# Token mixing: the normalised activations of successive tiles alternate between two buffers

## Chip, cores and metric

One Trainium2 chip; the kernel runs on 8 of its cores, and each core computes half of one batch element's tokens (4 batches, 2 halves). Nothing is exchanged between the cores. The metric is the device time in microseconds of the slowest core. Before the change it is 3632.73 us, the median of 3 runs (3630.87 to 3634.38).

## What is computed

The reference is a two-layer backbone. Each layer is a SwiGLU feed-forward, a token-mixing stage and a second feed-forward, each preceded by an RMS norm with scale and shift. Cut to the part that matters here, the mixing stage:

```python
n = norm_modulate(h, norm_mix[l], mx[:, 3], mx[:, 4])      # rmsnorm(h)*(1+scale)+shift
u, q, k, v = split(n @ w_in, [512, 1024, 1152])            # u 512, q 512, k 128, v 128 columns
pool_out = pool_mixer(u, w_pool, pool_scale)               # windowed means of u, minus u
q, k = apply_rope(q, cos, sin), apply_rope(k, cos, sin)
attn_out = latent_attention(q, k, v, kc, vc, sink)         # window of 128, plus context, plus sink
h = h + mx[:, 5] * (concat([pool_out, attn_out], -1) @ w_out)
```

Context tokens go through the same stage with their own scale and shift, so that a tile of columns can hold tokens of both kinds.

## The kernel before

The residual stream h lies in SBUF, transposed: 8 chunks (k) of 128 channels by 2560 token columns (2304 latent, 256 context). The program is a list of stages with a barrier over all engines between them; per layer they are feed-forward 1, the mixing stage (function mix), feed-forward 2. A small scheduler class records operations in the order in which the code is written, one queue for each engine, and derives semaphore waits from the names that an operation reads and writes. An engine executes its queue strictly in that order, so the order in the code is the order on each engine.

The change lies in the first phase of mix, called phase A here. It walks over five column tiles: four of 512 columns and a last one of 512 in layer 0 and 384 in layer 1. For each tile TensorE (PE) needs the normalised activations of all 8 chunks, kept in the buffer nTt (8 x 512, bf16). One tile's main steps are ten:

- 4 steps utok_step (u of 128 tokens: 8 matmuls of 512 columns, evacuated in turn by ScalarE, L513, and VectorE, L515), called **u blocks** here;
- 2 steps k_step (16 matmuls of 512 columns each, and then three VectorE operations L534, L536, L538 for the rotary embedding, called a **rope** here);
- 4 steps v_step (8 matmuls of 128 columns, evacuated by ScalarE, L547).

The last tile of layer 1 has three of the blocks of 128 tokens instead of four.

The normalisation of a tile is written as small steps. Eight **square** steps: a ScalarE square of one chunk (L346) and one PE matmul with a matrix of ones that adds up the channels, 512 columns. One **rstd** step: two ScalarE operations, Ln (L352) and Exp (L354). Then the **mod** steps: a VectorE multiplication h x rstd into one of two fp32 buffers tmp (L378), and a ScalarE operation that scales and shifts it into nTt (L380). There is one mod per chunk and kind of token: 8 in a tile of 512 latent columns, 24 in the last tile of layer 0 (latent, context, latent), 16 in the last tile of layer 1.

interleave(main, side) writes a main step, then a few side steps, then the next main step. Before the change the side list holds the 9 square and rstd steps of the next tile, one after each main step; the next tile's mods are written after the last main step, since they overwrite the only nTt that the v steps still read:

```python
                interleave(main, rn)
                for st in mn:
                    st()
```

After phase A comes the pooling phase: matmuls of u with the constant matrices in the buffer band (32 x 128, bf16, the same 8 KB per partition as nTt). Band is loaded by a DMA of POOL's queue at the head of the phase, behind the two loads of win (wkv, then wu), and is first read by the pooling phase.

Of the kernel before, what the change touches and what calls it, by code (L numbers as in the profile page):

```python
# [178 lines left out]
def build(upto="final", dump=False):  # L179
# [3 lines left out]
    with es:  # L183
        S = Sched(nc, es)

        def din(name, shape):
            return nc.dram_tensor(name, list(shape), F32, kind="ExternalInput").ap()
# [16 lines left out]
        bandT = din("bandT", [128, 32, 128])  # L204
# [45 lines left out]
        nTt = alloc(BF16, [8, 512], dma=True)  # L250
# [24 lines left out]
        band = alloc(BF16, [32, 128], dma=True)  # L275
# [90 lines left out]
        def norm_steps(c0, n, i_norm, dst, dst_keys, eng="dve", split=False):  # L366
            rsteps = rstd_steps(c0, n)
            steps = []
            shift_i = 3 * i_norm
            par = curp["par"]  # L370
            modraw, Amod = modraw_l[par], Amod_l[par]

            def mod_step(k, a, m, t):
                off = a - c0
                ti = cnt["tmp"] % 2
                cnt["tmp"] += 1
                tmp = tmp_s[ti]
                S.op(eng, lambda e: e.tensor_tensor(tmp[:, 0:m], hT[:, k, a:a + m], rstd[:, off:off + m], ALU.mult),  # L378
                     reads=hkeys(k, a, m) + [("rstd",)], writes=[("tmp", ti)])
                S.op("act", lambda e: e.activation(  # L380
                    dst(k, off, m), tmp[:, 0:m], AF.Identity, bias=modraw[:, shift_i * 8 + k, t:t + 1],
                    scale=Amod[:, i_norm, k, t:t + 1]),
                    reads=[("tmp", ti), ("modraw", par, shift_i), ("Amod", par, i_norm)], writes=dst_keys(k))

            for k in range(8):
                for (a, m, t) in colset_ranges(c0, n):
                    steps.append(lambda k=k, a=a, m=m, t=t: mod_step(k, a, m, t))
            if split:
                return rsteps, steps
            return rsteps + steps  # L390
# [5 lines left out]
        def interleave(main, side):  # L396
            side = list(side)
            nm = max(len(main), 1)
            per = (len(side) + nm - 1) // nm
            for st in main:  # L400
                st()
                for _ in range(per):
                    if side:
                        side.pop(0)()
            while side:
                side.pop(0)()
# [82 lines left out]
        def mix(l):  # L489
# [12 lines left out]

            S.dma("pool", None, wkv, win[l, :, :, 512:WCA], writes=[("wkv",)])
            S.dma("pool", None, wu, win[l, :, :, 0:512], writes=[("wu",)])
            S.dma("pool", None, band, bandT, writes=[("band",)])
            S.op("dve", lambda e: e.memset(Vaug[:, :, :, 64:128], 1.0), writes=[("Vaug",)])
            acols = [(0, 512), (512, 512), (1024, 512), (1536, 512), (2048, 384) if last else (2048, 512)]
            ev_i = [0]
# [5 lines left out]
                else:  # L514
                    S.op("dve", lambda e: e.tensor_copy(dst, src), reads=reads, writes=writes)  # L515

            def a_norm(c0, n):
                return norm_steps(c0, n, 1, lambda k, o2, m: nTt[:, k, o2:o2 + m], lambda k: [("nTt", k)], eng="dve", split=True)

            nk = [("nTt", k) for k in range(8)]  # L520
            r0, m0 = a_norm(*acols[0])
            for st in r0 + m0:
                st()
            for ti, (c0, n) in enumerate(acols):
                def cs_load(n=n, c0=c0):
                    S.dma("sp", None, cst[:, 0, 0:n], cosT[:, c0:c0 + n], writes=[("cs", 0)])
                    S.dma("sp", None, cst[:, 1, 0:n], sinT[:, c0:c0 + n], writes=[("cs", 1)])

                def k_step(g, n=n, c0=c0):
                    S.mm(pa[g][:, 0:n], [(wkv[:, k, g * 128:(g + 1) * 128], nTt[:, k, 0:n]) for k in range(8)],  # L530
                         reads=[("wkv",)] + nk, writes=[("pa", g)])
                    S.mm(pb[g][:, 0:n], [(wkv[:, k, 256 + g * 128:256 + (g + 1) * 128], nTt[:, k, 0:n]) for k in range(8)],
                         reads=[("wkv",)] + nk, writes=[("pb", g)])
                    S.op("dve", lambda e: e.tensor_tensor(rt[0][:, 0:n], pa[g][:, 0:n], cst[:, 0, 0:n], ALU.mult),  # L534
                         reads=[("pa", g), ("cs", 0)], writes=[("rt", 0)])
                    S.op("dve", lambda e: e.tensor_tensor(rt[1][:, 0:n], pb[g][:, 0:n], cst[:, 1, 0:n], ALU.mult),  # L536
                         reads=[("pb", g), ("cs", 1)], writes=[("rt", 1)])
                    S.op("dve", lambda e: e.tensor_tensor(kT[:, g, c0:c0 + n], rt[0][:, 0:n], rt[1][:, 0:n], ALU.add),  # L538
                         reads=[("rt", 0), ("rt", 1)], writes=[("kT", g, c0)])

                def v_step(tb, c0=c0):
                    blk = (c0 + tb * 128) // 128
                    pi = cnt["p"] % 2
                    cnt["p"] += 1
                    S.mm(py[pi][:, 0:128], [(nTt[:, k, tb * 128:(tb + 1) * 128], wkv[:, k, 512:640]) for k in range(8)],
                         reads=[("wkv",)] + nk, writes=[("py", pi)])
                    S.op("act", lambda e: e.copy(  # L547
                        Vaug[:, blk, :, 0:64], py[pi][:, 0:128].rearrange("p (g d) -> p g d", g=2)),
                        reads=[("py", pi)], writes=[("Vaug",)])

                def utok_step(tb, c0=c0):
                    blk = c0 // 128 + tb
                    pi = cnt["p"] % 2
                    cnt["p"] += 1
                    S.mm(py[pi][:, :], [(nTt[:, k, tb * 128:(tb + 1) * 128], wu[:, k, :]) for k in range(8)],
                         reads=[("wu",)] + nk, writes=[("py", pi)])
                    evac(utok[:, blk, :], py[pi][:, :], [("py", pi)], [("utok", blk)])

                cs_load()
                nb_ = n // 128  # L560
                main = [lambda tb=tb: utok_step(tb) for tb in range(nb_)]
                main += [lambda g=g: k_step(g) for g in range(2)]
                main += [lambda tb=tb: v_step(tb) for tb in range(nb_)]
                if ti + 1 < len(acols):
                    rn, mn = a_norm(*acols[ti + 1])
                else:
                    rn, mn = [], []
                interleave(main, rn)
                for st in mn:
                    st()  # L570
            oblocks = list(range(16)) if last else list(range(19))
            for t0 in range(0, len(oblocks), 4):
                obs = oblocks[t0:t0 + 4]
                n = 128 * len(obs)
# [96 lines left out]
            for ti, (c0, n) in enumerate(qtiles):  # L671
                S.dma("sp", None, cst[:, 0, 0:n], cosT[:, c0:c0 + n], writes=[("cs", 0)])
                S.dma("sp", None, cst[:, 1, 0:n], sinT[:, c0:c0 + n], writes=[("cs", 1)])
                nk = [("nTt", k) for k in range(8)]
# [38 lines left out]
                side = q_norm(*qtiles[ti + 1]) if ti + 1 < len(qtiles) else []  # L713
# [213 lines left out]
```

How the kernel before makes its waits and increments, by code:

```python
    def _waits(self, eng, d):  # L72
        seen = self.seen[eng]
        for s, v in d.items():
            if seen.get(s, 0) < v:
                seen[s] = v
                h = self.sems[s]
                self.ops[eng].append(lambda e, h=h, v=v: e.wait_ge(h, v))
# [10 lines left out]
    def op(self, eng, fn, reads=(), writes=()):  # L89
        self._waits(eng, self._deps(reads, writes))
        sname = "s_" + eng
        h = self.sem(sname)
        self.cnt[sname] += 1
        ev = (sname, self.cnt[sname])
        self.ops[eng].append(lambda e, fn=fn, h=h: fn(e).then_inc(h, 1))
        self.nins[eng] += 1
        self._commit(ev, reads, writes)
# [1 line left out]
    def mm(self, out, pairs, reads, writes, start=True, stop=True):  # L99
# [1 line left out]
        h = self.sem("s_pe")  # L101
        self.cnt["s_pe"] += 1
        ev = ("s_pe", self.cnt["s_pe"])
        n = len(pairs)
        for i, pr in enumerate(pairs):
            l, r = pr[0], pr[1]
            o_i = pr[2] if len(pr) > 2 else out
            st_i = pr[3] if len(pr) > 3 else (start and i == 0)
            sp_i = pr[4] if len(pr) > 4 else (stop and (i == n - 1))
            if i == n - 1:
                self.ops["pe"].append(lambda e, l=l, r=r, o_i=o_i, st_i=st_i, sp_i=sp_i: e.matmul(o_i, l, r, start=st_i, stop=sp_i).then_inc(h, 1))
            else:
                self.ops["pe"].append(lambda e, l=l, r=r, o_i=o_i, st_i=st_i, sp_i=sp_i: e.matmul(o_i, l, r, start=st_i, stop=sp_i))
        self.nins["pe"] += n
```

## Time and profile before

| what | value |
|---|---|
| median of 3 runs | 3632.73 us |
| the profiled execution, its own time | 3629.62 us |
| its span on the slowest core (core 3) | 3628.0 us |
| spans of the eight cores | 3610.2 to 3628.0 us |
| PE busy, share of the span | 3060.3 us, 84% |
| ACT busy (ScalarE) | 1096.0 us, 30% |
| DVE busy (VectorE) | 838.5 us, 23% |
| mean granted TensorE clock, core 3 | 0.924 |

PE is the matmul engine, PEld its weight load, ACT ScalarE, DVE VectorE, POOL GpSimd, SP the queue of plain DMAs. In a timeline a row is: start in us, us of the row's time, engine, line of the kernel, operation, destination <- source with shape, xcount, and in brackets the idle time of that engine before it with what ended it. Most tiles are called arena (SBUF) or ps (PSUM) by the profile, since the kernel carves them from one allocation each; lines tell them apart. All matmuls are recorded by one helper: L113 are those inside an accumulation group, L111 the last one of each group. A clock of 1.0 is 2.4 GHz and 0.5 is 1.2 GHz. In layer 0 phase A runs from about 735 to 927 us of the span, in layer 1 from about 2565 to 2740 us.

### The profile page before, as it was taken

What the parts mean: (1) busy time and instruction counts of PE and PEld (TensorE: products, weight loads), DVE (VectorE), ACT (ScalarE), POOL (GpSimd) and SP (SyncE); (2) the same over time, 40 slices, a digit from 0 to 9 for tenths busy, and PEclk for the clock granted to TensorE, in tenths of its full rate; (3) what the DMA queues carried; (4) which work ended last, traced back from release to release, by engine and by line L of the source; (5) the groups of instructions that cost most, each with busy time, mean ns of one, the idle gap of its engine ahead of it and who ended that gap; (6) DMA issues with size and microseconds to landing.
All of it is one profiled execution on the core that took longest, in us unless ns stands there. A gap on an engine that the chain in (4) does not pass through costs nothing.

```text
span 3628.0 us, 50030 instructions; the slowest of 8 cores (3610.2 to 3628.0 us)
## 1 busy us (share of the span) xinstructions
PE 3060.3 (84%) x17532; PEld 1545.9 (43%) x17532; DVE 838.5 (23%) x1491; ACT 1096.0 (30%) x1936; POOL 392.6 (11%) x560
## 2 busy tenths in 40 slices
PE   0799999955678877999998899999655888799997
PEld 0355555522333434555554454555323343344442
DVE  0212222123122222122122222221231222212113
ACT  0412311034345643122111313210343565312112
POOL 1011000000022220100100000000001322000000
PEclk9899999977589988999999999999886999899998
DMA  8565344230110004643743232343302000353444
GB/s 186 77 100 94 66 73 69 49 54 18 23 37 12 5 17 73 107 83 69 121 88 58 47 60 53 65 69 68 63 16 53 13 7 1 53 88 69 65 77 126
DMA packets 75957, 224.14 MB, mean 62 GB/s; under 512 B 9156, under 2 KB 14532, under 8 KB 74184
## 3 DMA queue, kind: packets, MB, share of 16 engines
q0 software_dynamic: 63328, 192.24, 31.6%
q1 hardware_dynamic: 12392, 28.70, 2.5%
q8 instruction: 153, 2.51, 0.3%
q14 instruction: 84, 0.69, 0.1%
HBM read 404.74 MB, written 8.39 MB: 114 GB/s over the span
## 4 chain that ended last, share of the span: by engine, by line
PE 73%; ACT 10%; issue 5%; DMA 5%; DVE 4%; POOL 3%; ACTq 0%; DVEq 0%; SPq 0%; POOLq 0%
PE ps L113 62%; PE ps L111 11%; ACT arena L634 3%; ACT arena L380 3%; POOL arena L686 2%; DMA arena<-win 2%; DVE arena L378 2%; DMA arena<-wmod 1%; ACT arena L651 1%; ACT arena L346 1%; DMA arena<-cT 1%; DMA arena<-wab 1%; DVE arena L682 1%; DMA arena<-wo 1%; DVE arena L723 0%
## 5 line engine op out<-in xcount | busy, mean ns | idle before, releaser
L113 PE MATMUL ps<-arena 128*128 128x512 bf16 (+3 forms) x15146 | 2813.8, 330 | 326.5 <-ACT arena L380 103.5
L113 PEld LDWEIGHTS ps<-arena 128*128 128x128 bf16 x15146 | 1349.1, 100 | 1567.5 <-issue 461.3
L111 PE MATMUL ps<-arena 128*128 128x512 bf16 (+3 forms) x2386 | 785.4, 341 | 230.8 <-ACT arena L346 186.8
L452 ACT ACTIVATE arena<-ps 128x512 f32<-128x512 f32 (+2 forms) x484 | 255.7, 529 | 1170.2 <-PE ps L111 1162.8
L454 DVE TENSOR_TENSOR arena<-arena,ps 128x512 bf16<-128x512 f32 (+2 forms) x484 | 291.4, 603 | 1151.6 <-PE ps L111 1114.0
L111 PEld LDWEIGHTS ps<-arena 128*128 128x128 bf16 x2386 | 237.9, 100 | 503.7 <-issue 368.2
L413 DVE SCALAR_TENSOR_TENSOR arena<-ps,arena 128x512 f32<-128x512 f32 (+3 forms) x288 | 175.3, 620 | 672.0 <-PE ps L111 672.0
L380 ACT ACTIVATE arena<-arena 128x512 bf16<-128x512 f32 (+3 forms) x392 | 265.3, 705 | 191.4 <-DVE arena L378 146.4
L346 ACT ACTIVATE arena<-arena 128x512 bf16<-128x512 f32 (+3 forms) x360 | 182.4, 579 | 318.2 <-DVE arena L413 199.3
L634 ACT ACTIVATE arena<-ps 128x512 bf16<-128x512 f32 x334 | 176.3, 598 | 202.9 <-PE ps L111 201.5
L378 DVE TENSOR_TENSOR arena<-arena 128x512 f32<-128x512 f32 (+3 forms) x312 | 164.4, 543 | 193.3 <-ACT arena L354 129.1
L131 POOL DMA_DIRECT2D arena<-wab x176 | 93.9, 534 | 891.5 <-PE ps L111 770.4
L131 POOL DMA_DIRECT2D arena<-wmod x144 | 76.8, 534 | 668.2 <-PE ps L111 656.3
L378 POOL TENSOR_TENSOR arena<-arena 128x512 f32<-128x512 f32 (+1 forms) x80 | 88.0, 1131 | 295.4 <-ACT arena L354 290.9
L658 DVE TENSOR_TENSOR arena<-ps,arena 64x256 bf16<-64x256 f32 x140 | 58.4, 417 | 264.7 <-ACT arena L652 257.4
L131 POOL DMA_DIRECT2D arena<-wo x64 | 33.9, 532 | 705.7 <-PE ps L111 705.7
L686 POOL TENSOR_TENSOR arena<-arena 64x512 bf16<-64x512 f32 (+1 forms) x72 | 88.6, 1230 | 112.5 <-DVE arena L682 109.8
L515 DVE CAST arena<-ps 128x512 bf16<-128x512 f32 (+1 forms) x37 | 25.3, 685 | 211.6 <-PE ps L111 211.6
L500 ACT ACT_TABLE_LOAD x2 | 2.6, 1283 | 191.3 <-DMA arena<-sinkrow 191.3
L131 POOL DMA_DIRECT2D arena<-win x6 | 5.3, 890 | 457.3 <-ACT arena L346 457.3
L680 DVE TENSOR_TENSOR arena<-ps,arena 128x512 f32<-128x512 f32 (+1 forms) x36 | 24.4, 677 | 122.1 <-POOL arena L686 76.0
L513 ACT CAST arena<-ps 128x512 bf16<-128x512 f32 (+1 forms) x38 | 22.0, 580 | 91.6 <-PE ps L111 91.5
(32 smaller groups left out, 314.7 us busy)
## 6 DMA issues: line engine op xcount, KB each, us to landing
arena<-wab POOLq DMA_DIRECT2D x176, 512.0 KB, 6.3
arena<-wo POOLq DMA_DIRECT2D x64, 704.0 KB, 6.6
arena<-wmod POOLq DMA_DIRECT2D x144, 256.0 KB, 5.2
arena<-xT SPq DMA_DIRECT2D x8, 1280.0 KB, 25.3
outT<-arena SPq DMA_DIRECT2D x32, 256.0 KB, 2.2
arena<-cosT SPq DMA_DIRECT2D x17, 256.0 KB, 2.7
arena<-sinT SPq DMA_DIRECT2D x17, 256.0 KB, 2.7
arena<-win POOLq DMA_DIRECT2D x2, 2048.0 KB, 17.2
```

Of the source, the lines that this page charges most:

```text
L111: self.ops["pe"].append(lambda e, l=l, r=r, o_i=o_i, st_i=st_i, sp_i=sp_i: e.matmul(o_i, l, r, start=st_i, stop=sp_i).then_inc(h, 1))
L113: self.ops["pe"].append(lambda e, l=l, r=r, o_i=o_i, st_i=st_i, sp_i=sp_i: e.matmul(o_i, l, r, start=st_i, stop=sp_i))
L131: self.ops[eng].append(lambda e: e.dma_start(out=out, in_=in_).then_inc(h, 16))
L346: S.op("act", lambda e: e.activation(sqr[si][:, 0:n], hT[:, k, c0:c0 + n], AF.Square), reads=hkeys(k, c0, n), writes=[("sq", si)])
L378: S.op(eng, lambda e: e.tensor_tensor(tmp[:, 0:m], hT[:, k, a:a + m], rstd[:, off:off + m], ALU.mult), reads=hkeys(k, a, m) + [("rstd",)], ...
L380: S.op("act", lambda e: e.activation(dst(k, off, m), tmp[:, 0:m], AF.Identity, bias=modraw[:, shift_i * 8 + k, t:t + 1], scale=Amod[:, i_n ...
L413: S.op("dve", lambda e, a=a, m=m, t=t, o2=o2: e.scalar_tensor_tensor(hT[:, d, a:a + m], pst[1][:, o2:o2 + m], gate[:, i_norm, d, t:t + 1], ...
L452: S.op("act", lambda e, pi=pi, n=n: e.activation(sa_s[pi][:, 0:n], pa[pi][:, 0:n], AF.Silu), reads=[("pa", pi)], writes=[("sa", pi)])
L454: S.op("dve", lambda e, pi=pi, n=n, j=j, off=off: e.tensor_tensor(gTb[:, j, off:off + n], sa_s[pi][:, 0:n], pb[pi][:, 0:n], ALU.mult), rea ...
L634: S.op("act", lambda e, stp=stp, pti=pti: e.activation(PT[pti], stp[:, :], AF.Exp, scale=0.125), reads=[stkey], writes=[("PT", pti)])
L658: S.op("dve", lambda e, i0v=i0v, i1v=i1v, ov=ov: e.tensor_tensor(ov, i0v, i1v, ALU.mult), reads=[pvkey, ("rt", 0)], writes=[("aot", 2 * g) ...
L686: S.op("pool", lambda e, c=c, n=n, hf=hf, rows=rows: e.tensor_tensor(qz[rows, 2 * c + hf, 0:n], rt[0][rows, 0:n], rt[1][rows, 0:n], ALU.ad ...
```

## The change

The tiles alternate between two buffers: even tiles are normalised into nTt as before, odd tiles into nTt2, which is the memory of band seen as 8 x 512. The next tile's normalisation, all of it, becomes the side list of the present tile: 17 steps over ten main steps, so two after each main step until they are used up; 33 in the last transition of layer 0 (four after each) and 25 in that of layer 1 (three after each). The load of band moves behind the tile loop. Its writers and readers of the odd tiles share one name, ("band",), where nTt has one name per chunk.

```diff
-            S.dma("pool", None, band, bandT, writes=[("band",)])
...
-            def a_norm(c0, n):
-                return norm_steps(c0, n, 1, lambda k, o2, m: nTt[:, k, o2:o2 + m], lambda k: [("nTt", k)], eng="dve", split=True)
+            nTt2 = band.rearrange("p a b -> p (a b)").rearrange("p (k c) -> p k c", k=8)
+            nbufs = [nTt, nTt2]
+
+            def nkeys(ti):
+                return [("nTt", k) for k in range(8)] if ti % 2 == 0 else [("band",)]
+
+            def a_norm(ti, c0, n):
+                nb = nbufs[ti % 2]
+                return norm_steps(c0, n, 1, lambda k, o2, m: nb[:, k, o2:o2 + m],
+                                  (lambda k: [("nTt", k)]) if ti % 2 == 0 else (lambda k: [("band",)]), eng="dve")
...
-                if ti + 1 < len(acols):
-                    rn, mn = a_norm(*acols[ti + 1])
-                else:
-                    rn, mn = [], []
-                interleave(main, rn)
-                for st in mn:
-                    st()
+                side = a_norm(ti + 1, *acols[ti + 1]) if ti + 1 < len(acols) else []
+                interleave(main, side)
+            S.dma("pool", None, band, bandT, writes=[("band",)])
```

The matmuls of k, v and u read whichever of the two buffers holds their tile. Three places show what moves. On VectorE, the rows of the first tile of layer 0 before the change: two evacuations of u (L515), two ropes (L534, L536, L538), then the eight multiplications of the next tile's mods (L378).

```order
L515 CAST arena<-ps 128x512 x2
L534 TENSOR_TENSOR arena<-ps,arena 128x512
L536 TENSOR_TENSOR arena<-ps,arena 128x512
L538 TENSOR_TENSOR arena<-arena 128x512
L534 TENSOR_TENSOR arena<-ps,arena 128x512
L536 TENSOR_TENSOR arena<-ps,arena 128x512
L538 TENSOR_TENSOR arena<-arena 128x512
L378 TENSOR_TENSOR arena<-arena 128x512 x8
```

The same place with the change (the lines are 1 lower for the evacuation, L514, and 7 higher for the rope, L541, L543, L545):

```order
L514 CAST arena<-ps 128x512 x2
L541 TENSOR_TENSOR arena<-ps,arena 128x512
L543 TENSOR_TENSOR arena<-ps,arena 128x512
L545 TENSOR_TENSOR arena<-arena 128x512
L378 TENSOR_TENSOR arena<-arena 128x512
L541 TENSOR_TENSOR arena<-ps,arena 128x512
L543 TENSOR_TENSOR arena<-ps,arena 128x512
L545 TENSOR_TENSOR arena<-arena 128x512
L378 TENSOR_TENSOR arena<-arena 128x512 x7
```

One mod stands between the two ropes; seven still stand behind the second rope. On ScalarE, the same tile with the change (L512 evacuates u, L554 v):

```order
L512 CAST arena<-ps 128x512
L346 ACTIVATE arena<-arena 128x512 x4
L512 CAST arena<-ps 128x512
L346 ACTIVATE arena<-arena 128x512 x4
L352 ACTIVATE arena<-ps,arena 128x512
L354 ACTIVATE arena<-arena 128x512
L380 ACTIVATE arena<-arena 128x512 x3
L554 CAST arena<-ps 128x2x64
L380 ACTIVATE arena<-arena 128x512 x2
L554 CAST arena<-ps 128x2x64
L380 ACTIVATE arena<-arena 128x512 x2
L554 CAST arena<-ps 128x2x64
```

Before, the squares stood as 2, 4, 1 and 1 between the evacuations, and all eight L380 behind the fourth evacuation of v. Now all eight squares come in the four u blocks, and the evacuations of v stand among the mods. On POOL the load of band keeps its place in the queue and gets waits for ScalarE and PE:

```order
L131 DMA arena<-win 128x8x640
L131 DMA arena<-win 128x8x512
L131 DMA arena<-bandT 128x4096 [waits s_act,s_pe]
```

Before, the third of these rows had no wait. The waits are for the last mod into band and the last matmul that reads it, the fourth v step of the fourth tile.

## Rows read from the trace of the kernel before

**Rows 1.** The page's head.

```profile
span 3628.0 us, 50030 instructions; the slowest of 8 cores (3610.2 to 3628.0 us)
```

**Rows 2.** Busy time by stage: second, fourth, last tile (layer 0), fourth, last (layer 1).

```profile
core 3: us, PE busy (x) PEld busy (x) DVE busy (x) ACT busy (x) POOL busy (x), PEclk, DMA share, GB/s
798.20:832.26 34.06, 20.40 (x105) 9.66 (x105) 10.99 (x16) 13.61 (x24) 0.00 (x0) 0.80 0.05 16
866.33:908.67 42.34, 20.33 (x104) 9.56 (x105) 13.53 (x32) 20.01 (x40) 0.00 (x0) 0.74 0.05 13
908.67:927.30 18.63, 18.46 (x95) 8.64 (x96) 5.54 (x8) 1.82 (x5) 0.00 (x0) 0.85 0.00 1
2689.86:2725.85 35.99, 19.19 (x105) 9.12 (x106) 10.94 (x24) 14.43 (x32) 0.00 (x0) 0.83 0.04 11
2725.85:2739.97 14.12, 13.96 (x81) 7.31 (x81) 4.04 (x7) 1.70 (x4) 0.00 (x0) 0.85 0.00 0
```

**Rows 3.** Waits in phase A of layer 0: us in total, times, longest.

```profile
PE ps L113 <- ACT arena L380: 44.1, 4, 17.2
```

**Rows 4.** Timeline of PE, second tile of layer 0, and the third tile's start.

```profile
798.20 3.15 PE L113 MATMUL ps<-arena 128*128 128x512 bf16 x7 [9.20 <-ACT arena L380]
...
803.09 0.38 PE L111 MATMUL ps<-arena 128*128 128x512 bf16 x1 [1.35 <-ACT arena L346]
...
810.65 1.67 PE L113 MATMUL ps<-arena 128*128 128x512 bf16 x7
...
814.32 1.67 PE L113 MATMUL ps<-arena 128*128 128x512 bf16 x7
...
832.26 3.14 PE L113 MATMUL ps<-arena 128*128 128x512 bf16 x7 [8.85 <-ACT arena L380]
```

**Rows 5.** Timeline of ScalarE in the same tile.

```profile
801.83 0.58 ACT L513 CAST arena<-ps 128x512 bf16<-128x512 f32 x1 [3.88 <-PE ps L111]
802.31 1.15 ACT L346 ACTIVATE arena<-arena 128x512 bf16<-128x512 f32 x2
...
822.71 0.27 ACT L547 CAST arena<-ps 128x128 bf16<-128x128 f32 x1 [1.30 <-PE ps L111]
822.87 0.69 ACT L352 ACTIVATE arena<-ps,arena 128x512 f32<-128x512 f32 x1
...
825.17 1.52 ACT L380 ACTIVATE arena<-arena 128x512 bf16<-128x512 f32 x2 [0.74 <-DVE arena L378]
```

**Rows 6.** Timeline of VectorE in the same tile.

```profile
812.72 0.69 DVE L534 TENSOR_TENSOR arena<-ps,arena 128x512 f32<-128x512 f32 x1 [1.32 <-PE ps L111]
...
815.24 0.69 DVE L538 TENSOR_TENSOR arena<-arena 128x512 bf16<-128x512 f32 x1
...
818.84 0.69 DVE L538 TENSOR_TENSOR arena<-arena 128x512 bf16<-128x512 f32 x1
824.38 1.29 DVE L378 TENSOR_TENSOR arena<-arena 128x512 f32<-128x512 f32 x2 [4.85 <-ACT arena L354]
826.16 1.40 DVE L378 TENSOR_TENSOR arena<-arena 128x512 f32<-128x512 f32 x2 [0.48 <-ACT arena L380]
```

**Rows 7.** VectorE: first mod of the last tile, layer 0, then layer 1.

```profile
892.45 0.63 DVE L378 TENSOR_TENSOR arena<-arena 128x128 f32<-128x128 f32 x2 [4.76 <-ACT arena L354]
...
2714.60 0.63 DVE L378 TENSOR_TENSOR arena<-arena 128x128 f32<-128x128 f32 x2 [4.17 <-ACT arena L354]
```

**Rows 8.** PE in the first tile of layer 0: second u block, fourth v step.

```profile
767.22 3.19 PE L113 MATMUL ps<-arena 128*128 128x512 bf16 x7
...
787.94 0.95 PE L113 MATMUL ps<-arena 128*128 128x128 bf16 x7
```

**Rows 9.** Timeline, first tile of layer 0: its last mods, its first matmuls.

```profile
755.58 1.52 ACT L380 ACTIVATE arena<-arena 128x512 bf16<-128x512 f32 x2 [0.25 <-DVE arena L378]
...
761.81 3.14 PE L113 MATMUL ps<-arena 128*128 128x512 bf16 x7 [14.01 <-DMA arena<-win]
```

**Rows 10.** DMA issues, 735 to 770 us: count, KB each, us to landing.

```profile
arena<-bandT POOLq DMA_DIRECT2D x1, 1024.0 KB, 24.3
```

**Rows 11.** The page's DMA issues: the nearest smaller load of POOL's queue.

```profile
arena<-wo POOLq DMA_DIRECT2D x64, 704.0 KB, 6.6
```

More of the change, by code:

```diff
@@ L515, in evac @@
                     S.op("dve", lambda e: e.tensor_copy(dst, src), reads=reads, writes=writes)
-            def a_norm(c0, n):
-                return norm_steps(c0, n, 1, lambda k, o2, m: nTt[:, k, o2:o2 + m], lambda k: [("nTt", k)], eng="dve", split=True)
-            nk = [("nTt", k) for k in range(8)]
-            r0, m0 = a_norm(*acols[0])
-            for st in r0 + m0:
+            nTt2 = band.rearrange("p a b -> p (a b)").rearrange("p (k c) -> p k c", k=8)
[6 more added lines that the diff above has]
+                                  (lambda k: [("nTt", k)]) if ti % 2 == 0 else (lambda k: [("band",)]), eng="dve")
+            for st in a_norm(0, *acols[0]):
                 st()
             for ti, (c0, n) in enumerate(acols):
+                nTt_ = nbufs[ti % 2]
+                nk = nkeys(ti)
                 def cs_load(n=n, c0=c0):
@@ L527, in cs_load, with k_step @@
                     S.dma("sp", None, cst[:, 1, 0:n], sinT[:, c0:c0 + n], writes=[("cs", 1)])
-                def k_step(g, n=n, c0=c0):
+                def k_step(g, n=n, c0=c0, nTt=nTt_, nk=nk):
                     S.mm(pa[g][:, 0:n], [(wkv[:, k, g * 128:(g + 1) * 128], nTt[:, k, 0:n]) for k in range(8)],
@@ L539, in k_step, with v_step @@
                          reads=[("rt", 0), ("rt", 1)], writes=[("kT", g, c0)])
-                def v_step(tb, c0=c0):
+                def v_step(tb, c0=c0, nTt=nTt_, nk=nk):
                     blk = (c0 + tb * 128) // 128
@@ L549, in v_step, with utok_step @@
                         reads=[("py", pi)], writes=[("Vaug",)])
-                def utok_step(tb, c0=c0):
+                def utok_step(tb, c0=c0, nTt=nTt_, nk=nk):
                     blk = c0 // 128 + tb
```

## The prediction, made before the changed kernel ran

> **What bounds the kernel now.** I read the page's head first, then the waits of phase A, then its time by stage, and last one tile engine by engine. The span is 3628.0 us on the slowest core [rows 1], and the change touches phase A alone, twice. There the view of waits has one entry that the change can remove: before four tiles of layer 0, PE's first matmul waits for the next tile's last mod, 44.1 us in all, 17.2 the longest [rows 3]. Tiles are serial: a regular transition takes 34.06 us, of which PE is busy 20.40; the transition into the last tile takes 42.34 in layer 0 and 35.99 in layer 1 [rows 2]. In the timeline PE stands 9.20 and 8.85 us before two tiles [rows 4], while VectorE and ScalarE work off eight mods: from 824.38 [rows 6] to 832.26 [rows 4], 7.88 us. A pair of mods takes 826.16 - 824.38 = 1.78 us, so one takes 0.89: two tmp buffers make VectorE and ScalarE alternate.
>
> **A regular transition, step by step.** There are six (three per layer). All offsets are from the tile's first matmul, 798.20 [rows 4].
>
> *The front gets later.* After a u block, ScalarE evacuates it, squares, and PE's matmul with ones waits for that: 1.35 us [rows 4]. With two squares per block PE waits for the second one too. Two squares take 1.15 us, the first about 0.6, so the second adds 0.53 [rows 5]. ScalarE evacuates two of the four blocks, so this happens twice; behind the other two the squares are ready. Further, four ones matmuls move ahead of the k steps, two of them without any wait to hide in: 17 matmuls take 814.32 - 810.65 = 3.67 us, 0.216 each [rows 4]. Together 2 x 0.53 + 2 x 0.216 = 1.5 us: the first k step moves from offset 12.45 (810.65) to 13.95. The second follows after 16 matmuls instead of 17, 3.46 us later: 17.41.
>
> *The ropes.* The first rope ends 815.24 + 0.69 - 810.65 = 5.28 us after its k step's start [rows 4, 6], at 19.23. The one mod that now stands between the ropes fits there: rstd is ready 824.38 - 822.87 = 1.51 us after Ln starts [rows 5, 6], and Ln can start at about 14.2, behind the last ones matmul, so at 15.7. It delays the second rope's first operation by half a microsecond, but not its second, which waits for PE anyway. The second rope ends 818.84 + 0.69 - 814.32 = 5.21 us after its k step [rows 4, 6]: 22.62.
>
> *The tail.* Seven mods remain: from 22.7, 7 x 0.89 = 6.2 plus what the eight of before took beyond 8 x 0.89 (0.76) is 7.0, so 29.7. Two things may stretch this. ScalarE's mods into band now each wait for the one before (one name for all chunks), and three evacuations of v stand among them. From below: nothing, since in a cycle of 1.78 a pair keeps ScalarE busy for 1.52 [rows 5]. From above: three evacuations at 0.25 each, 0.75, as one takes 0.27 [rows 5]. I take 0.3, nearer the first, because the pair's slack holds one evacuation. The next tile starts at 30.0 instead of 34.06: **4.06 us gained, six times: 24.4.** PE's third and fourth v step now wait for evacuations behind mods, which costs nothing: they end before the last mod.
>
> **The last transitions.** Layer 0: four squares stand behind each of the first two u blocks. The evacuation starts at 3.63 (801.83), takes 0.58, four squares 2.2, so PE resumes at 6.75; a u block (1.73) and four ones matmuls (0.86) bring 9.34, the third block 11.07, its evacuation 11.9, rstd 13.4. From there VectorE works off the train of 24 mods, 908.67 - 892.45 = 16.22 us [rows 2, 7], with one evacuation (0.69) and six rope operations (4.5 with gaps) put into it: 34.8, less 0.4 where VectorE need not wait for ScalarE behind an interruption: 34.4. **42.34 - 34.4 = 7.9.** Layer 1: the first mod stands behind the fourth u block's evacuation, about offset 14.6; the train is 2725.85 - 2714.60 = 11.25 us [rows 2, 7], with the same six rope operations 30.4, a little less for the same reason, 30.3. **35.99 - 30.3 = 5.7.** I allow 0.8 either way on each. The first tile's own normalisation and the last tile's matmuls keep their order: nothing.
>
> **The load of band**, moved. Behind nothing but its wait in POOL's queue, it is issued after the fourth tile's fourth v step. That step waits for an evacuation that stands five mods (layer 0) or four (layer 1) ahead of the last: about 31.2 and 28.0. The last tile takes 18.63 and 14.12 us [rows 2] from 34.4 and 30.3, so the load has some 21.8 and 16.4 us. Its price alone is in no row. From below 6.6 us, as a smaller load of that queue took [rows 11]; from above 24.3, band's own landing behind two loads of win [rows 10]. I take about 9, since nothing else is in that queue then: hidden by the last tile, nothing to pay. At the upper end 2.5 + 7.9 = 10.4 us would show. At the phase's head band no longer follows win: PE's start there waits for win until 761.81 though the mods end at 757.10 [rows 9], so at most 4.7 us, and 5.0 with a little in layer 1; at least nothing, which I take, as band was issued behind win.
>
> The load's descriptors are now made beside VectorE's casts. The Trainium skill (SBUF — State Buffer, Who interferes with whom) says that some casts and copies take the port pair that GpSimd needs, so that a load issued by POOL stands still behind them. No row here shows such a stall; by the rule the load is late by part of VectorE's work. For a bound from rows: all of that work in the last tile of layer 0 is 5.54 us [rows 2], and 9 + 5.5 still lands in time.
>
> **The clock.** Each tile starts at 1.2 GHz: seven matmuls of 512 columns take 3.15 us against 1.67 later [rows 4]. In the first tile of layer 0 the second u block was at 1.2 GHz too, 3.19 [rows 8]: 1.5 us more. The wait behind the first block grows by half a microsecond, so some more second blocks may start at 1.2 GHz. Eight tiles (four per layer) have that wait; on this core only the one shown did so. Bounds: none more, or all seven others: 10.6. I take two more, as the wait grows by less than half: 3.0 us lost. The first block stays at 1.2 GHz: the fourth v step was at that level after two waits of some 1 us (0.95 us for seven short matmuls) [rows 8], and from the third v step to the next tile PE will again do almost nothing. The Trainium skill (TensorE: Matmul & The Clock Gate, HAM oscillation) says that an idle stretch which is short enough leaves the clock up. By that rule the shorter stretch could start tiles at 2.4 GHz; that is the second rival.
>
> **Sum.** 24.4 + 7.9 + 5.7 - 3.0 = 35.0. The profiled execution took 3629.6 us, so 3594.6; the median of the three runs is 3.1 above it, so **3598 us** (-1.0%). No later stage gets other work or another order, so nothing is given back there.
>
> **Rivals.**
> 1. *The whole tile at 1.2 GHz (slower than before).* If the longer waits keep the clock down through all u and k blocks, 56 of a tile's 64 matmuls of 512 columns take 0.21 us more (1.48 / 7), 11.8 us per tile; eight tiles 94 us against 38 gained: 3689. It decides from some 23 extra slow matmuls per tile. Against it: 32 matmuls of the k steps follow without a wait. For it: only that two long waits stand in each tile.
> 2. *Tiles start at 2.4 GHz.* Each of the eight transitions gains another 8 x 0.21 = 1.7, and the 3.0 lost fall away: 38 + 13.5 = 51.5 gained: 3581. Against it: [rows 8].
> 3. *Band lands late*, 10.4 us in all: 3608. For it: eight cores load at the same time; against: nothing stands in front of it in its queue.
> 4. *The second u block is slow in every tile*: 7.6 us less gain, 3605.
> 5. *The change does not do what it says*: seven of eight mods still stand behind the second rope. If ScalarE's queue (evacuations, waits on its own mods) stretches each mod by 0.5 us, 3.5 us per regular transition, about all is eaten: six times 3.5 is 21, leaving 14: 3619. Against it: the slack of 0.25 per pair.
>
> **How the numbers follow.** About 0.2% (7.3 us) is what a measurement can tell from no change. Chances: forecast 0.70, rival 1 0.03, rival 2 0.08, rival 3 0.07, rival 4 0.08, rival 5 0.04. The forecast's own range: up by 0.3 x 6 = 1.8, 1.6, 3.0 and 5.0 to 3587; down by 2.7, 1.6 and 7.6 to 3610. To hold 8 in 10, with rivals 3 and 4 inside, I give 3583 to 3612. All but rival 1 are faster by over 0.2%; with a little for what I don't see: faster 0.94, same 0.03, slower 0.03.
>
> **What would show it.** Right: a regular transition of 30 us, the last ones 34 and 30; one L378 between the ropes, then seven; PE's waits for L346 twice per tile, about 1.9 us; PE's wait for the last mod down from 8.9 to some 2 us; no wait of PE for bandT. Wrong: u or k blocks at 3.1 us throughout, a wait for bandT before the pooling phase, mods at more than 0.9 us each, or a tile whose k steps start later than offset 14.5.

## The result, and the profile after

The changed kernel takes 3595.29 us (median), the kernel before, run beside it, 3632.74. Four of the nine runs behind this median, and two of the ten before, were slowed by a lower granted clock on one die or on both; the ratio, taken from the others (3592.84 to 3595.29 us after the change), is 0.9896, with a 95% interval from 0.9883 to 0.9908: 1.04% faster. 3598 had been predicted, and 3594.6 for the profiled execution, which took 3594.31.

The page's head, which answers to [rows 1], and the busy time:

```profile
span 3592.7 us, 50089 instructions; the slowest of 8 cores (3574.6 to 3592.7 us)
...
PE 3071.0 (85%) x17532; PEld 1545.4 (43%) x17532; DVE 835.5 (23%) x1491; ACT 1095.2 (30%) x1936; POOL 392.6 (11%) x560
```

The slowest core is now core 6; before it was core 3. What follows is core 3's, as in [rows 2 to 7], unless another is named. The span of core 3 fell from 3628.0 to 3588.1, 39.9 us, and the mean over the eight cores from 3619.7 to 3584.8, 34.9. Core 6 gained less than core 3: from 3626.2 to 3592.7.

Busy time by stage, to be read beside [rows 2]: the second and the fourth tile of layer 0, the fourth and the last tile of layer 1. The columns are those of [rows 2].

```profile
789.01:818.77 29.76, 21.02 (x104) 9.67 (x105) 10.71 (x16) 13.45 (x24) 0.00 (x0) 0.84 0.07 18
850.01:882.79 32.78, 20.94 (x104) 9.80 (x105) 12.66 (x32) 19.47 (x40) 0.55 (x1) 0.81 0.06 17
2655.65:2685.62 29.97, 20.75 (x105) 9.72 (x106) 10.37 (x24) 14.29 (x32) 0.55 (x1) 0.84 0.05 14
2685.62:2699.80 14.18, 13.96 (x75) 7.02 (x75) 3.94 (x7) 1.62 (x4) 0.00 (x0) 0.83 0.40 75
```

The engines do the same work in less time: 34.06 became 29.76, 42.34 became 32.78, 35.99 became 29.97. The last tile, 14.12 before, stayed at 14.18. All eight transitions of core 3, from the first matmul of a tile to that of the next:

| transition | before | after | gained |
|---|---|---|---|
| layer 0, first | 36.39 | 30.14 | 6.25 |
| second | 34.06 | 29.76 | 4.30 |
| third | 34.07 | 31.24 | 2.83 |
| last | 42.34 | 32.78 | 9.56 |
| layer 1, first | 34.36 | 29.58 | 4.78 |
| second | 34.05 | 29.79 | 4.26 |
| third | 34.20 | 31.28 | 2.92 |
| last | 35.99 | 29.97 | 6.02 |
| sum | 285.46 | 244.54 | 40.9 |

The sum is core 3's whole gain in span, 39.9, and one more. Over the eight cores the transitions shrank by 37.5 us on average, the spans by 34.9. So the gain lies in the transitions. Most of the other 2.6 us are given back in the next phase of the stage, where PE waits for its own load of win (the q columns). Core 3 in layer 0, before and after:

```profile
1003.94 3.15 PE L113 MATMUL ps<-arena 128*128 128x512 bf16 x7 [15.29 <-DMA arena<-win]
979.91 3.14 PE L113 MATMUL ps<-arena 128*128 128x512 bf16 x7 [17.34 <-DMA arena<-win]
```

Over the eight cores PE's wait at this place grew from 13.9 to 15.8 us on average in layer 0 and from 12.9 to 13.7 in layer 1, in one profiled execution each; where win is early, it is 12.5 and ends with the phase's own mods. Why it grew was not tried.

The waits of PE in phase A of layer 0, after (us in total, times, longest):

```profile
PE ps L113 <- ACT arena L554: 28.9, 12, 6.2
PE ps L111 <- ACT arena L346: 17.2, 8, 7.7
PE ps L113 <- DMA arena<-win: 13.5, 1, 13.5
```

The entry of [rows 3], 44.1 us of waiting for mods, is gone by name. In its place the profile has twelve waits for evacuations of v (L554), which now stand between and behind the mods in ScalarE's queue. Eight of the twelve, 21.5 us, are those of the third and fourth v steps. The other four, 7.4 us, stand at the starts of tiles, and there the name misleads: by the code a tile's first u block needs the last mod, but not the last evacuation. ScalarE at the end of the second tile, before and after:

```profile
830.49 1.52 ACT L380 ACTIVATE arena<-arena 128x512 bf16<-128x512 f32 x2 [0.25 <-DVE arena L378]
...
817.71 0.81 ACT L380 ACTIVATE arena<-arena 128x512 bf16<-128x512 f32 x1
818.43 0.25 ACT L554 CAST arena<-ps 128x128 bf16<-128x128 f32 x1
```

PE starts the next tile 0.25 us after the end of the last mod, in the kernel before (832.01, 832.26) as with the change (818.52, 818.77), and so at the other tile starts of this core. So the tiles are still serial, and PE still waits for the last mod, but 7.4 us instead of 44.1. The waits for squares (L346) are fewer too: 17.2 us in 8 times, where the kernel before had 28.1 in 17.

PE in the second tile of layer 0, the tile of [rows 4]:

```profile
789.01 3.14 PE L113 MATMUL ps<-arena 128*128 128x512 bf16 x7 [1.94 <-ACT arena L554]
...
793.93 0.90 PE L111 MATMUL ps<-arena 128*128 128x512 bf16 x2 [1.35 <-ACT arena L346]
794.73 1.67 PE L113 MATMUL ps<-arena 128*128 128x512 bf16 x7
...
803.03 1.67 PE L113 MATMUL ps<-arena 128*128 128x512 bf16 x7
...
806.48 1.67 PE L113 MATMUL ps<-arena 128*128 128x512 bf16 x7
...
814.31 0.91 PE L113 MATMUL ps<-arena 128*128 128x128 bf16 x7 [3.32 <-ACT arena L554]
...
816.08 0.91 PE L113 MATMUL ps<-arena 128*128 128x128 bf16 x7 [0.76 <-ACT arena L554]
...
818.77 3.15 PE L113 MATMUL ps<-arena 128*128 128x512 bf16 x7 [1.68 <-ACT arena L554]
```

The first k step starts at offset 14.02 (803.03), the second at 17.47 (806.48). Before the next tile PE waits 1.68 us where it had waited 8.85. VectorE in the same tile, to be read beside [rows 6]:

```profile
807.62 0.69 DVE L545 TENSOR_TENSOR arena<-arena 128x512 bf16<-128x512 f32 x1
808.23 0.68 DVE L378 TENSOR_TENSOR arena<-arena 128x512 f32<-128x512 f32 x1
808.83 0.68 DVE L541 TENSOR_TENSOR arena<-ps,arena 128x512 f32<-128x512 f32 x1
...
811.00 0.69 DVE L545 TENSOR_TENSOR arena<-arena 128x512 bf16<-128x512 f32 x1
811.61 1.29 DVE L378 TENSOR_TENSOR arena<-arena 128x512 f32<-128x512 f32 x2
...
816.92 0.69 DVE L378 TENSOR_TENSOR arena<-arena 128x512 f32<-128x512 f32 x1 [0.37 <-ACT arena L380]
```

One mod stands between the ropes, and it costs the second rope nothing. That rope ends at 811.69, offset 22.68, and the other seven mods follow at once; before, VectorE idled 4.85 us there for rstd [rows 6]. From the rope's end to the next tile is 7.08 us. The load of band, in the DMA issues of layer 0, answers to [rows 10]:

```profile
arena<-bandT POOLq DMA_DIRECT2D x1, 1024.0 KB, 9.9
```

POOL issues it at offset 31.10, and it lands in 9.9 us. Over all cores and both layers it takes 8.0 to 9.9, fourteen of sixteen loads at most 8.6, and nobody waits for it.

### The profile page after: what moved, and what is told of

It reads as the page before. It is cut to its first block, busy times and chain, and to the rows that moved or that the text cites. A ratio compares the mean times of both kernels' runs of the same rounds, so it can differ in the third digit from the quotient of the medians.

```text
span 3592.7 us, 50089 instructions; the slowest of 8 cores (3574.6 to 3592.7 us)
## 1 busy us (share of the span) xinstructions
PE 3071.0 (85%) x17532; PEld 1545.4 (43%) x17532; DVE 835.5 (23%) x1491; ACT 1095.2 (30%) x1936; POOL 392.6 (11%) x560
## 4 chain that ended last, share of the span: by engine, by line
PE 73%; ACT 9%; issue 5%; DMA 5%; DVE 4%; POOL 3%; ACTq 0%; DVEq 0%; SPq 0%; POOLq 0%
PE ps L113 63%; PE ps L111 10%; ACT arena L637 3%; POOL arena L689 2%; ACT arena L380 2%; DMA arena<-win 2%; DVE arena L378 1%; DMA arena<-wmod 1%; ACT arena L654 1%; DMA arena<-cT 1%; ACT arena L346 1%; DMA arena<-wab 1%; DVE arena L685 1%; DVE arena L726 0%; ACT arena L512 0%
## 5 line engine op out<-in xcount | busy, mean ns | idle before, releaser
L380 ACT ACTIVATE arena<-arena 128x512 bf16<-128x512 f32 (+3 forms) x392 | 267.4, 706 | 233.6 <-DVE arena L378 187.0
L346 ACT ACTIVATE arena<-arena 128x512 bf16<-128x512 f32 (+3 forms) x360 | 180.5, 578 | 317.4 <-PE ps L111 116.4
L378 DVE TENSOR_TENSOR arena<-arena 128x512 f32<-128x512 f32 (+3 forms) x312 | 163.9, 542 | 159.3 <-ACT arena L354 95.6
L378 POOL TENSOR_TENSOR arena<-arena 128x512 f32<-128x512 f32 (+1 forms) x80 | 88.0, 1131 | 294.7 <-ACT arena L354 290.7
L514 DVE CAST arena<-ps 128x512 bf16<-128x512 f32 (+1 forms) x37 | 25.3, 684 | 220.7 <-PE ps L111 220.7
L352 ACT ACTIVATE arena<-ps,arena 128x512 f32<-128x512 f32 (+3 forms) x45 | 29.2, 649 | 77.2 <-PE ps L111 72.5
L512 ACT CAST arena<-ps 128x512 bf16<-128x512 f32 (+1 forms) x38 | 22.0, 579 | 90.6 <-PE ps L111 90.5
```

Source lines behind the costliest of these rows:

```text
L346: S.op("act", lambda e: e.activation(sqr[si][:, 0:n], hT[:, k, c0:c0 + n], AF.Square), reads=hkeys(k, c0, n), writes=[("sq", si)])
L380: S.op("act", lambda e: e.activation(dst(k, off, m), tmp[:, 0:m], AF.Identity, bias=modraw[:, shift_i * 8 + k, t:t + 1], scale=Amod[:, i_n ...
```

## The experiments

The expectations name theories by letter. A: the gain is the order alone, since rstd and one mod come ahead of the second rope and the tile is one serial chain, so that whatever shortens this chain gains again. B: part of the gain lies at the head of the phase, where band no longer follows win in its queue. C: the second buffer as such gains, since a mod need not wait for the last reader of the only one. D: an earlier front gains nothing, since the work behind it sets the end of the tile.

**The load of band alone.** The kernel before, with only that load moved:

```diff
-            S.dma("pool", None, band, bandT, writes=[("band",)])
...
+                if ti == 3:
+                    S.dma("pool", None, band, bandT, reads=[("kT", 1, c0)], writes=[("band",)])
```

> The kernel before, with one part of the change alone: the load of band is issued behind the fourth tile's second rope instead of at the head of phase A; one buffer, the old order of steps. Theory A (the gain is the reordered normalisation): transitions stay at 34.06 and 42.3 us, the first tile starts when win has landed as before, band lands some 8 to 9 us after its issue and nobody waits for it; 3632 us within 4. Theory B (part of the gain comes from the head, where band no longer competes with win): win lands earlier in layer 0, up to 4.7 us, so 3627 to 3629.

Measured: ratio 1.0007 (0.9965 to 1.005). The interval is too wide to exclude the 5.0 us that the prediction had as its upper bound, so the trace has to speak. The DMA issues of layer 0 on the slowest core (core 2):

```profile
arena<-win POOLq DMA_DIRECT2D x1, 1280.0 KB, 15.1
arena<-win POOLq DMA_DIRECT2D x1, 1024.0 KB, 19.3
arena<-bandT POOLq DMA_DIRECT2D x1, 1024.0 KB, 8.3
```

The kernel before shows 15.0 and 20.4 for the two loads of win. In layer 0 PE's wait for win is 13.2 us on average over the eight cores, 14.4 before and 13.3 after the change; the second load lands after 18.6 us instead of 20.0. In layer 1 it lands after 16.6, and 16.4 before. So taking band away from behind win gives about one microsecond in layer 0 and nothing in layer 1. The transitions keep the lengths of before (36.4, 34.1, 34.1 and 42.4 on core 1). B falls but for this microsecond; the next experiment, which has the late load too, has a lower end of the interval of 0.9992, so that 2.9 us are the most that the late load and the second buffer can give together. Band alone in its queue lands in 8.0 to 9.2 us over all cores.

**The second buffer alone.** The changed kernel with the order of before: the mods are written behind the last main step.

```diff
-                side = a_norm(ti + 1, *acols[ti + 1]) if ti + 1 < len(acols) else []
-                interleave(main, side)
+                rn, mn = a_norm(ti + 1, *acols[ti + 1]) if ti + 1 < len(acols) else ([], [])
+                interleave(main, rn)
+                for st in mn:
+                    st()
```

> The changed kernel with both buffers and the late band load, but the order of before: nine side steps among the main steps, the next tile's mods behind the fourth v step. Theory A: rstd is still only ready behind the third v step, so the second buffer frees the mods of nothing but the wait for the fourth v step, less than half a microsecond: regular transitions 33.6 to 34.1 us, the last of layer 0 42 us, 3626 to 3633 us. Rival C (the overwritten buffer was what held the mods back): most of the gain stays, 3595 to 3605 us.

Measured: ratio 1.0005 (0.9992 to 1.0017). VectorE on core 0, second tile of layer 0:

```profile
812.83 0.69 DVE L546 TENSOR_TENSOR arena<-arena 128x512 bf16<-128x512 f32 x1
818.32 1.29 DVE L378 TENSOR_TENSOR arena<-arena 128x512 f32<-128x512 f32 x2 [4.80 <-ACT arena L354]
```

The 4.80 us of idling for rstd are back, and PE stands 9.12 us before the next tile. The transitions of this core in layer 0 are 34.75, 34.31, 34.44 and 42.12. The buffer alone gains nothing: before the change the mods were held by rstd, not by the readers of nTt. It is what allows the other order. C falls.

**One name for eight chunks.** The prediction put 0.3 us per transition on two things, one of them that mods into band wait for each other. Here the odd buffer has one name per chunk, and the load of band writes all of them:

```diff
-            return [("nTt", k) for k in range(8)] if ti % 2 == 0 else [("band",)]
+            return [("nTt", k) for k in range(8)] if ti % 2 == 0 else [("n2", k) for k in range(8)]
...
-                                  (lambda k: [("nTt", k)]) if ti % 2 == 0 else (lambda k: [("band",)]), eng="dve")
+                                  (lambda k: [("nTt", k)]) if ti % 2 == 0 else (lambda k: [("n2", k)]), eng="dve")
...
-            S.dma("pool", None, band, bandT, writes=[("band",)])
+            S.dma("pool", None, band, bandT, writes=[("band",)] + [("n2", k) for k in range(8)])
```

> The changed kernel with one name per chunk for the second buffer, so that a mod into band no longer waits for the mod before it. Theory A (that wait costs a part of a microsecond per transition into band, beside the evacuations of v): the seven mods behind the second rope take 7.2 us into both buffers instead of 7.4 to 7.7 into band and 7.2 into nTt; four transitions, 1 to 2 us in all: 3593 to 3595 us, no difference that a timing shows. Rival: it costs nothing (trains stay as they are). Rival above: it costs 1.2 us each, 5 us in all: 3590 us.

Measured: ratio 0.9886 (0.9844 to 0.9929), which can't be told from the change's 0.9896. ScalarE in core 6, a pair of mods into band, first in the changed kernel:

```profile
845.29 1.72 ACT L380 ACTIVATE arena<-arena 128x512 bf16<-128x512 f32 x2 [2.63 <-DVE arena L378]
```

and with a name per chunk:

```profile
781.83 1.52 ACT L380 ACTIVATE arena<-arena 128x512 bf16<-128x512 f32 x2
```

The second mod of a pair no longer waits for the end of the first, 0.2 us. On this core the stretch from the second rope to the next tile shrinks from 7.30 to 7.08 us where band is the target (in the first tile of layer 0 from 7.65 to 7.44), and stays at 7.08 where nTt is. The wait is real, and worth 0.22 us in four of the eight transitions: 0.9 us, too little to be seen in the time.

**Squares two ahead.** The changed kernel, with each square written two steps ahead of its matmul with ones, and the first two ahead of the tile (sq_act is the ScalarE part of a square step):

```diff
+                if ahead and k + ahead < 8:
+                    sq_act(k + ahead)
...
+            if ahead:
+                steps.insert(0, lambda: [sq_act(j) for j in range(ahead)])
...
+                side = a_norm(ti + 1, *acols[ti + 1], ahead=2) if ti + 1 < len(acols) else []
+                if side:
+                    side.pop(0)()
```

> The changed kernel with ScalarE's squares written two ahead of the matmuls with ones that read them, so that PE finds them ready and does not wait for evacuation and squares behind the first and third u block. Theory A (these waits make the front of a tile later and bring a second u block at 1.2 GHz): the waits of PE for L346 fall away, the first k step starts at offset 10.3 to 10.8 instead of 14 to 15, and the rest follows: regular transitions 26 to 27 us, the last ones 3 us shorter, some 28 to 35 us in all: 3560 to 3568 us. Rival D (ScalarE and VectorE bound the tile, PE's waits are slack): transitions stay within a microsecond of 30 to 31 us, 3590 to 3596 us.

Measured: ratio 0.981 (0.9781 to 0.9838), against 0.9896 for the change. PE on core 4, second tile of layer 0:

```profile
787.16 2.76 PE L113 MATMUL ps<-arena 128*128 128x512 bf16 x6 [2.32 <-ACT arena L569]
789.72 1.48 PE L111 MATMUL ps<-arena 128*128 128x512 bf16 x3
791.00 1.78 PE L113 MATMUL ps<-arena 128*128 128x512 bf16 x7
...
813.98 1.49 PE L113 MATMUL ps<-arena 128*128 128x512 bf16 x3 [2.33 <-ACT arena L569]
```

Both waits of 1.35 us are gone, and the second u block is no longer at 1.2 GHz (1.78 us for seven). This tile takes 26.82 us, 2.94 less than the 29.76 that core 3 took with the change and without a slow second block; twice 1.35 is 2.7. So the front is on the path, as A says, and D falls. The last transition of layer 0 gained only 1.3 us (32.78 to 31.47), where 3 had been expected: there the train of 24 mods sets the end.

**Mods ahead of the ropes.** k_step is split into its matmuls and its rope, and all mods are written between the k matmuls and the v steps:

```diff
-                main += [lambda g=g: k_step(g) for g in range(2)]
-                main += [lambda tb=tb: v_step(tb) for tb in range(nb_)]
...
-                interleave(main, side)
+                interleave([lambda tb=tb: utok_step(tb) for tb in range(nb_)], rn[:8])
+                for st in rn[8:]:
+                    st()
+                for g in range(2):
+                    k_step(g)
+                for st in mn:
+                    st()
+                for tb in range(nb_):
+                    v_step(tb)
+                for g in range(2):
+                    rope(g)
```

> The changed kernel with the next tile's rstd and all its mods written behind the k steps' matmuls but ahead of both ropes and of the v steps; two squares per u block as in the change. Theory A (VectorE's strict order, seven mods behind the second rope, sets the tile): the first mod starts when rstd is ready, at offset 16 to 17 instead of 19 to 23, eight mods take 7.9 to 8.1 us, then the evacuations of v; regular transitions 25 to 26.5 us instead of 29.7 to 31.3, the last of layer 0 unchanged (its train of 24 already started early), that of layer 1 27 to 28; some 31 to 36 us in all: 3559 to 3565 us. Rival D (ScalarE's queue bounds the tile, or the ropes, now later, hold up the next tile): transitions stay at 29 us or more, 3585 to 3596 us.

Measured: ratio 0.9768 (0.9751 to 0.9785); the median, 3548.0 us, lies below what A had expected. PE on core 4, from the end of the first tile of layer 0 to the start of the third:

```profile
784.48 0.55 PE L113 MATMUL ps<-arena 128*128 128x128 bf16 x7 [2.27 <-ACT arena L557]
...
784.92 0.90 PE L113 MATMUL ps<-arena 128*128 128x128 bf16 x7
...
785.75 2.97 PE L113 MATMUL ps<-arena 128*128 128x512 bf16 x7
...
809.11 0.55 PE L113 MATMUL ps<-arena 128*128 128x128 bf16 x7 [1.83 <-ACT arena L557]
...
810.38 1.67 PE L113 MATMUL ps<-arena 128*128 128x512 bf16 x7 [0.22 <-PE ps L111]
```

The order gives what it should: this tile takes 24.63 us. Two things change with it, which this run does not separate: the mods come ahead of the ropes on VectorE, and all of them ahead of v's evacuations on ScalarE. What came on top is in part the clock. In the four transitions of layer 0 PE on core 3 is busy for 76.86 us at a clock of 0.94, where the change had 84.40 at 0.84. On average over the cores the transitions of both layers gained 40.7 us on the change and the spans 48.1; the 7.4 outside the transitions were not followed. On core 4 the second tile starts at 1.2 GHz (2.97 us for seven), the third at 2.4 (1.67), behind a wait of 1.83 instead of 2.27 us. Over the cores the mean granted clock is 0.935 to 0.942, against 0.925 to 0.930 for the change. This is the mechanism of the prediction's second rival, which the change itself never reached: there the first block was at 1.2 GHz in all 64 transitions of the eight cores (3.14 or 3.15 us on core 3). The rule that the prediction cites from the Trainium skill (TensorE: Matmul & The Clock Gate, HAM oscillation), by which a short enough idle stretch leaves the clock up, agrees with these rows of core 4: 1.83 us left it up, 2.27 did not. Other cores stayed up behind 2.27 us too (last section), so that the length of the wait alone does not decide.

**Both.** The last two edits together.

> Both reorderings together: squares two ahead of the matmuls with ones, and mods ahead of the ropes. Theory A (the two act on different parts of the chain, front and tail, and add): the first mod at offset 12.4, regular transitions 21 to 22 us, the last of layer 0 29 to 30, of layer 1 24 to 25; 3525 to 3533 us. Rival: they overlap, because PE's own 20 us of matmuls per tile plus the wait for v's evacuations then bound the tile: transitions 24 to 25 us, 3545 to 3552 us.

Measured: ratio 0.969 (0.9673 to 0.9707). Against the change's 0.9896 the squares gave 0.0086 and the mods 0.0128, together 0.0214; both give 0.0206, so they add up. PE on core 0:

```profile
782.50 1.99 PE L113 MATMUL ps<-arena 128*128 128x512 bf16 x6 [0.22 <-PE ps L111]
...
801.24 0.55 PE L113 MATMUL ps<-arena 128*128 128x128 bf16 x7 [1.83 <-ACT arena L572]
...
802.73 1.46 PE L113 MATMUL ps<-arena 128*128 128x512 bf16 x6 [0.43 <-ACT arena L572]
```

A tile takes 20.23 us, and PE is busy in 17.91 of them. The time is some 10 us better than expected, and the clock is again higher than with the change (0.935 to 0.942).

**Both, and u's weights first.** The two loads of win exchanged, since u blocks come first in a tile:

```diff
-            S.dma("pool", None, wkv, win[l, :, :, 512:WCA], writes=[("wkv",)])
             S.dma("pool", None, wu, win[l, :, :, 0:512], writes=[("wu",)])
+            S.dma("pool", None, wkv, win[l, :, :, 512:WCA], writes=[("wkv",)])
```

> As the run before, with the two loads of win exchanged at the head of the phase, the u columns first, since the first block of a tile reads only these. Theory A (a load lands behind what was issued ahead of it): the first tile of a layer starts when its own mods end, up to 5 us earlier in layer 0 and half a microsecond in layer 1: 3520 to 3531 us. Rival: both loads land together late, nothing gained, 3525 to 3533 us.

Measured: ratio 0.967 (0.9647 to 0.9694). The DMA issues of layer 0 on the slowest core:

```profile
arena<-win POOLq DMA_DIRECT2D x1, 1280.0 KB, 19.8
arena<-win POOLq DMA_DIRECT2D x1, 1024.0 KB, 14.0
```

The load of u's columns (1024 KB) lands after 14.0 us instead of 19.4, and PE's wait for win, 13.4 us on this core in the run before, is gone from the list of waits; in its place PE waits 9.4 us for the first tile's own mods. By time the gain over the run before is 5 us of medians (3518.8 to 3513.5), and the intervals of the two overlap. So the earlier landing is shown by the rows, the gain in time is not. This version has the lowest ratio, 3.3% below the kernel before, where the change alone gives 1.0%.

## Why the prediction was right, point by point

**The front.** It had the first k step at offset 13.95, the second at 17.41 and the second rope's end at 22.62; the profile shows 14.02, 17.47 and 22.68. The two extra squares per tile that PE waits for and the two uncovered ones matmuls were the right terms. Only how the wait would show was wrong: "about 1.9 us" is in the profile a wait of 1.35 and, behind it, a pair of matmuls that takes 0.90.

**The tail.** 7.0 and 0.3 had been put behind the second rope; measured on core 3 are 7.08 into nTt and 7.30 into band (7.65 in the first tile of layer 0). So the evacuations of v cost nothing that can be seen, as they fit the slack, and the shared name costs 0.22, which the third experiment shows. PE's wait for the last mod fell to 1.5 to 2.2 us, as predicted (some 2). A regular transition without a cold second block takes 29.6 to 30.1 us on core 3; 30.0 was predicted.

**The last transition of layer 0** was mis-sized: 34.4 predicted, 32.78 measured, 1.6 us too pessimistic. The first mod came as predicted (863.33, offset 13.32, against 13.4). What failed is the term "one evacuation (0.69) and six rope operations (4.5 with gaps) put into it", less 0.4. VectorE on core 3 around the first rope in that train:

```profile
867.01 0.29 DVE L378 TENSOR_TENSOR arena<-arena 128x128 f32<-128x128 f32 x1 [0.49 <-ACT arena L380]
867.22 0.68 DVE L541 TENSOR_TENSOR arena<-ps,arena 128x512 f32<-128x512 f32 x1
867.83 0.68 DVE L543 TENSOR_TENSOR arena<-ps,arena 128x512 f32<-128x512 f32 x1
868.61 0.69 DVE L545 TENSOR_TENSOR arena<-arena 128x512 bf16<-128x512 f32 x1
869.22 0.62 DVE L378 TENSOR_TENSOR arena<-arena 128x256 f32<-128x256 f32 x2
```

In the undisturbed train VectorE waits for ScalarE before nearly every mod. During a rope ScalarE catches up, so that the mods behind it (869.22, two of them) need no wait. The train took 882.79 - 863.33 = 19.46 us, 3.24 more than the 16.22 of [rows 2, 7], where 4.8 had been added. In layer 1 the same term was nearer: 30.3 predicted, 29.97 measured.

**The clock.** Two more second u blocks at 1.2 GHz, 3.0 us, had been put. On core 6, the slowest, five of the eight tiles have a slow second block, such as

```profile
825.53 1.10 PE L111 MATMUL ps<-arena 128*128 128x512 bf16 x2 [1.35 <-ACT arena L346]
826.43 2.66 PE L113 MATMUL ps<-arena 128*128 128x512 bf16 x7
```

The five take 2.78, 2.66, 3.19, 2.79 and 2.66 us, 5.7 more than five at 1.67. This core had two before the change (3.03 us in the later one), so it lost some 2.8 more. On core 3 the two third transitions (31.24 and 31.28) have one each, and the first tile, which had one before [rows 8], has none. That the first block stays at 1.2 GHz was right: 3.15 us at the tile starts shown. Rivals 1 and 2 did not come; rival 4, a slow second block in every tile, came in five of eight tiles on core 6 and in two on core 3.

**The load of band** was issued at offsets 31.10 and 28.96 (31.2 and 28.0 predicted) and landed in 8.0 to 9.9 us (9 taken), inside the last tile. By the Trainium skill's rule on shared ports (SBUF — State Buffer, Who interferes with whom), which the prediction named, some of VectorE's casts could hold the load up. The load takes some 8 us beside the casts and ropes of the last tile, and as long in the first experiment, beside mods; a load with VectorE at rest was not tried. In the last three experiments the same load takes 8.1 to 12.7 us, and what stretches it there was not tried either. So no run here shows whether the rule bears on this load. Late it is nowhere. Rival 3 falls, and so does rival 5: three pairs of mods take 816.92 - 811.61 = 5.31 us, 0.885 each.

**The head** at zero was right within about a microsecond (first experiment).

**The sum.** 35.0 predicted, 35.3 between the two profiled executions. This agreement is partly luck. The sentence that no later stage gives anything back was wrong: the wait before the next phase's first matmul, mostly for its load of win, took back 2.7 us on average over the cores (1.86 and 0.85), a term that the prediction had at nothing; and the transitions gained 37.5 on average, 2.5 more than the sum had for them. Core 3, for which the sum was made, gained 39.9: 1.7 more than predicted on the last transition of layer 0, 0.3 on that of layer 1, 0.2 to 0.7 on each regular one, and less lost to the clock (twice some 1.3 in the third transitions, less the 2 us of the slow block that the first tile had before). The time is that of the slowest core, which is another one now, and which gained 33.5.

## What to carry to other kernels

A second buffer gains by the order that it permits, not by itself: look for what held the work back (here rstd, which was written late, so that the buffer alone gave 0), and move that first. In queues that run strictly in order, what many wait for goes ahead of what only the next stage needs: squares before they are asked for and mods ahead of ropes took the ratio from 0.9896 to 0.969, twice the change's own gain, without any further memory. When an operation is put into a train of two engines that wait for each other in turn, it can cost less than its own length, since waits around it vanish: 3.24 us here, in the one train where it was measured, for seven operations put at 4.8.

## What was not expected of the hardware

The wait before a tile does not tell by itself at which level the tile starts. In the run with the mods ahead of the ropes, all eight cores wait 2.26 or 2.27 us before the third v step of the first tile of layer 0. On cores 0, 2 and 6 the next tile then started at 2.4 GHz; on the five others the clock fell before it did. Core 2, to be read beside core 4 above:

```profile
782.79 0.55 PE L113 MATMUL ps<-arena 128*128 128x128 bf16 x7 [2.26 <-ACT arena L557]
...
784.06 1.67 PE L113 MATMUL ps<-arena 128*128 128x512 bf16 x7 [0.22 <-PE ps L111]
```

One tile later, behind 1.83 or 1.84 us, all eight cores stayed up. In layer 1 five of eight stayed up behind 2.55 us, and one of eight fell behind 2.12. In the changed kernel core 3 was at 1.2 GHz right behind a wait of 3.32 us (0.91 for the seven short matmuls), but not behind 3.57 in the tile before (0.55); from the next wait on it was at 1.2 in both. So the shortest of these waits left all cores up, and the longer ones left some up and not others, with the same instructions. In a tile that starts at 1.2 GHz it is alike: the second block is slow on one core and fast on another (2.66 and 1.67 us) behind the same wait of 1.35. What tells these apart was not tried; with the squares ahead, and that wait gone, the block shown took 1.78.
